# A decoder layer with 32 experts: two spare places for expert weights, emptied by GpSimd's copies

## The reference, cut to what matters

```python
SEQ, D_MODEL, N_EXPERTS, TOP_K = 256, 1024, 32, 4

def reference(x, c, positions, ...):
    mod = silu(c) @ ada_w + ada_b                  # six rows: shift, scale, gate, twice
    h = rms_norm(x) * (1 + scale1) + shift1
    x = x + gate1 * rms_norm(hybrid_mixer(h, ...))
    h = rms_norm(x) * (1 + scale2) + shift2
    x = x + gate2 * rms_norm(moe_ffn(h, ...))
    return x

def moe_ffn(h, ...):
    top_val, top_idx = top_k(h @ w_router + b_router, 4)
    weight = softmax(top_val)
    # for each expert e and its tokens:
    #   hu = h[tokens] @ w_up[e] + b_up[e]         # 1024 x 2048, 8 MB
    #   a  = clamped_swiglu(hu)
    #   out[tokens] += weight * (a @ w_down[e] + b_down[e])   # 1024 x 1024, 4 MB
```

## Time and profile before

| | us |
|---|---|
| median of 3 runs | 1294.62 (1293.81 to 1295.19) |
| the profiled execution | 1292.38 |
| its span, first to last instruction | 1290.2 |
| TensorE busy in the span | 1123.2 |
| SyncE's queue: 460.98 MB | 85.4% of the 16 DMA engines |
| VectorE, ScalarE, GpSimd busy | 316.0, 314.2, 0.2 |

### The profile page before, as it was taken

How to read it: one execution, slowest core, us unless ns; L and a number is a source line. 1 busy time by engine, 2 the same in 40 slices (tenths; PEclk the granted TensorE clock), 3 DMA queues, 4 the chain that set the end, 5 groups by cost and what they waited for, 6 DMA issues and landing times.

```text
span 1290.2 us, 20882 instructions
## 1 busy us (share of the span) xinstructions
PE 1123.2 (87%) x7942; PEld 569.1 (44%) x7943; DVE 316.0 (24%) x802; ACT 314.2 (24%) x589; POOL 0.2 (0%) x4
## 2 busy tenths in 40 slices
PE   6999999998998669988988989979978688687785
PEld 4745788753444233443343443433433334233332
DVE  3045463462221110312121211212111112111112
ACT  2145422032222221112122221222222122222213
POOL 0000000000000000000000000000000000000000
PEclk9999999998999889989999999999999899899898
DMA  9932664553899999469999999999999999999995
GB/s 381 428 130 98 275 279 186 216 217 151 315 419 428 428 428 370 177 240 429 426 429 428 429 428 428 429 428 430 427 430 429 429 427 428 430 427 429 429 429 249
DMA packets 33740, 464.89 MB, mean 360 GB/s; under 512 B 4002, under 2 KB 4130, under 8 KB 5540
## 3 DMA queue, kind: packets, MB, share of 16 engines
q1 hardware_dynamic: 32688, 460.98, 85.4%
q10 hardware_dynamic: 1012, 3.34, 0.7%
HBM read 463.25 MB, written 1.05 MB: 360 GB/s over the span
## 4 chain that ended last, share of the span: by engine, by line
PE 58%; DMA 37%; DVE 3%; issue 1%; SPq 0%; ACT 0%; DVEq 0%; ACTq 0%
DMA ring<-in_w_up 33%; PE psum L972 20%; PE psum L595 17%; PE psum L1049 8%; DMA ring<-in_w_down 3%; PE psum L900 3%; PE psum L964 2%; PE psum L1067 2%; DMA ring<-in_ada_quarters 1%; PE psum L661 1%; DVE area L1754 1%; PE psum L601 1%; PE psum L947 1%; DVE area L1725 0%; PE psum L891 0%
## 5 line engine op out<-in xcount | busy, mean ns | idle before, releaser
L972 PE MATMUL psum<-ring,area 128*32 128x512 f32 (+2 forms) x2432 | 391.3, 632 | 77.9 <-DMA ring<-in_w_up 77.9
L972 PEld LDWEIGHTS psum<-ring,area 128*32 128x32 f32 (+2 forms) x2432 | 107.3, 122 | 352.0 <-issue 228.7
L1049 PE MATMUL psum<-ring,area 128*32 128x256 f32 (+2 forms) x2080 | 191.3, 419 | 23.6 <-DVE area L1739 14.8
L900 PEld LDWEIGHTS psum<-area,x_res 128*128 128x128 f32 x1056 | 124.5, 196 | 33.8 <-issue 33.8
L900 PE MATMUL psum<-area,x_res 128*128 128x128 f32 x1056 | 131.2, 283 | 1.7 <-DVE area L1634 1.7
L1049 PEld LDWEIGHTS psum<-ring,area 128*32 128x32 f32 (+2 forms) x2080 | 75.9, 115 | 128.4 <-issue 66.3
L1260 ACT ACTIVATE area<-area 128x256 f32<-128x256 f32 x51 | 21.3, 417 | 420.5 <-DVE area L1714 420.5
L1714 DVE TENSOR_SCALAR area<-psum 128x256 f32<-128x256 f32 x51 | 21.7, 425 | 405.6 <-PE psum L972 405.6
L1219 ACT ACTIVATE area<-psum,mod,small 128x128 f32<-128x128 f32 (+1 forms) x272 | 101.7, 455 | 58.2 <-PE psum L900 55.1
L1248 ACT ACT_TABLE_LOAD x32 | 41.1, 1283 | 281.9 <-PE psum L947 281.9
L595 PE MATMUL psum<-ring,hT 128*128 128x512 f32 (+1 forms) x192 | 77.5, 559 | 0.0
(11 more groups left out here) (201 smaller groups left out, 632.9 us busy)
## 6 DMA issues: line engine op xcount, KB each, us to landing
ring<-in_w_up SPq DMA_DIRECT2D x128, 2048.0 KB, 22.2
ring<-in_w_down SPq DMA_DIRECT2D x64, 2048.0 KB, 22.5
ring<-in_w_in SPq DMA_DIRECT2D x10, 2048.0 KB, 16.0
ring<-in_ada_w SPq DMA_DIRECT2D x8, 2048.0 KB, 13.1
ring<-in_ada_quarters SPq DMA_DIRECT2D x4, 2048.0 KB, 18.0
ring<-in_w_out SPq DMA_DIRECT2D x2, 2048.0 KB, 10.0
ring<-in_w_in SPq DMA_DIRECT2D x4, 512.0 KB, 18.7
ring<-in_w_branch_b SPq DMA_DIRECT2D x1, 2048.0 KB, 9.3
```

Source lines behind the costliest of these rows:

```text
L900: ins = pe.matmul(ps[banks[i]][:, kk % 4 * P:(kk % 4 + 1) * P], x3[:, tt, kk * P:(kk + 1) * P], S[:, tt, 0:P], start=(tt == 0 and kk % 4 = ...
L972: ins = pe.matmul(ps[b][g * P // G:(g + 1) * P // G, 0:w], XT[:, kk, t0:t0 + P // G], wt[:, c0:c0 + w], start=False, stop=kk == KT - 1, sk ...
L1049: ins = pe.matmul(ps[b][g * M:(g + 1) * M, 0:w], hidT[:, p, q * P + of * M:q * P + (of + 1) * M], down_weights(kk)[:, g * W + d * CW:g * W ...
```

## The change

Two places of 2 MB are added, `extra[0]` and `extra[1]`. The first lies over `hT` and the start of `arena`, the second over another part of `arena` with `ybT` and `silu_rep`, which are not used in the expert loop; the tiles that the loop does use are moved behind (`S`, `Sg`, `GT`, `xw` and the router's), and `area` grows.

For places 1, 2, 7 and 8 the first two pairs of `w_up` are loaded into the spare places, and for places 1 and 7 both halves of `w_down` after them. GpSimd copies each into its slot of the ring once that is free, in eight copies of 128x512, and raises the semaphore that TensorE waits for anyway. Pairs 2 and 3 go to the ring directly as before, and so do all loads of the other places. `UP_BY_WAY` and `DOWN_BY_WAY` hold, for each such place, how many times the spare place was emptied before.

```diff
+UP_BY_WAY = {1: 0, 2: 2, 7: 3, 8: 5}
+DOWN_BY_WAY = {1: 1, 7: 4}
...
-        area = sb("area", TT * D + 14848)
+        area = sb("area", TT * D + KT * T + 14848 + 2048)
...
+        extra = [area[:, TT * D:TT * D + KT * CW], arena[:, 8192:8192 + KT * CW]]
...
+            un.wait_full(sp, "logit1")
+
+            def up_by_way(number, e):
                 for j in range(2):
+                    if UP_BY_WAY[e]:
+                        sp.wait_ge(extra_read[j], UP_BY_WAY[e])
+                    sp.dma_start(extra[j], a["w_up"][ds(number, 1), j, :, :].rearrange("e p n -> p (e n)")
+                                 ).then_inc(extra_full[j], 16)
+
+            def up_rest(number, e):
+                sp.wait_ge(up_used, (KT - 2) * e)
+                up_load(number, 2)
+                sp.wait_ge(up_full, MAX_U * e)
+                up_load(number, 3)
+
+            def down_by_way(number, e):
+                for j in range(2):
+                    sp.wait_ge(extra_read[j], DOWN_BY_WAY[e])
+                    sp.dma_start(extra[j], a["w_down"][ds(number, 1), j, :, :].rearrange("e p n -> p (e n)")
+                                 ).then_inc(extra_full[j], 16)
...
+            two_by_way(1)
+            direct(3, 7)
+            two_by_way(7)
+            direct(9, E)
...
+        @block.gpsimd
+        def _(gp):
+            def moved(j, to, landed):
+
+                for c in range(KT):
+                    ins = gp.tensor_copy(to[:, c * CW:(c + 1) * CW], extra[j][:, c * CW:(c + 1) * CW])
+                ins.then_inc(landed, 16)
+
+            for e in sorted(UP_BY_WAY):
+                for j in range(2):
+                    gp.wait_ge(extra_full[j], 16 * (UP_BY_WAY[e] + 1))
+                    gp.wait_ge(up_used, (KT - 2) * (e - 1) + 2 * j + 2)
+                    moved(j, slot(NF + j), up_pair[j])
+                    gp.wait_ge(up_pair[j], 16 * e + 16)
+                    gp.sem_inc(extra_read[j], 1)
+                if e not in DOWN_BY_WAY:
+                    continue
+                for j in range(2):
...
```

More of the change, by code:

```diff
@@ L207, in layer_kernel @@
         x_res = sb("x_res", TT * D)
-        hT = sb("hT", KT * T)
-        area = sb("area", TT * D + 14848)
+        area = sb("area", TT * D + KT * T + 14848 + 2048)
         yaT = sb("yaT", 2 * T)
-        ybT = sb("ybT", 4 * T)
         grow = sb("grow", D)
         late = sb("late", LATE_W)
-        silu_rep = sb("silu_rep", KT * 32)
         mod = sb("mod", 48)
@@ L222, in layer_kernel @@
         xn = area[:, 0:TT * D]
-        arena = area[:, TT * D:]
+        hT = area[:, TT * D:TT * D + KT * T]
+        arena = area[:, TT * D + KT * T:]
+        ybT, silu_rep = arena[:, 10752:10752 + 4 * T], arena[:, 11776:11776 + KT * 32]
+        extra = [area[:, TT * D:TT * D + KT * CW], arena[:, 8192:8192 + KT * CW]]
         cols = cst[:, C_COLS:C_COLS + R_N]
@@ L259, in layer_kernel @@
         sbT = region(8704, (8, T))
-        gates = region(10752, (16, T))
-        sbw = region(10752, (10, TRI))
+        gates = region(12288, (16, T))
+        sbw = region(12288, (10, TRI))
         prob = xn[:, 0:NG * P + NG * T]
@@ L289, in layer_kernel @@
         Y = hid
[L290 to L293, removed]
+        S = region(16384, (TT, T))
+        Sg = region(12288, (2, TT * P))
+        GT = region(12800, (2, T))
+        xw = region(13312, (8, T))
         pick = yaT[:, :].rearrange("p (c m) -> p c m", c=4)
[L295 to L303, removed]
+        lg = region(15360, (8, TT * E))
+        posm = region(15872, (TT, E + 1))
+        gate = region(15872 + 2 * (E + 1), (TT, E + 1))
+        top = region(15872 + 4 * (E + 1), (TT, 8))
+        posm2 = region(15872 + 4 * (E + 1) + 16, (TT, E + 1))
+        posm64 = rope[:, 0:TT * (E + 1)].rearrange("p (x y) -> p x y", x=TT)
+        gT = region(16128, (T,))
+        gate4 = region(13312, (TT, P))
         ada_sums = [grow[:, 0:CW], grow[:, CW:D]] + [region(i * CW, (CW,)) for i in (0, 1, 2, 3, 8, 9)]
@@ L350, in layer_kernel @@
         up_used, dn_used = sem("up_used"), sem("dn_used")
+        extra_full, extra_read = ([sem(f"{n}{j}") for j in range(2)] for n in ("extra_full", "extra_read"))
         xe_full, xe_read = sem("xe_full"), sem("xe_read")
@@ L563, in _ @@
             sp.wait_ge(order_ready, 1)
[L564 to L571, removed]
-                for j in range(2):
[L573 to L577, removed]
+            un.wait_full(sp, "logit1")
@@ new lines, in down_by_way, with down_direct @@
+            def down_by_way(number, e):
[3 more added lines that the diff above has]
+                                 ).then_inc(extra_full[j], 16)
+            def down_direct(number, e):
+                sp.wait_ge(dn_used, (FT // 2 - 1) * e - (FT // 2 - 1) + 2)
+                down_load(number, 0)
+                sp.wait_ge(dn_full, MAX_D * e)
+                down_load(number, 1)
@@ new lines, in direct, with two_by_way @@
+            def direct(first, last):
+                with sp.Fori(first, last) as e:
+                    number = expert_at(sp, e)
+                    for j in range(KT // 2):
+                        if j < KT // 2 - 1:
+                            sp.wait_ge(up_used, (KT - 2) * e - (KT - 2) + 2 * j + 2)
+                        else:
+                            sp.wait_ge(up_full, MAX_U * e)
+                        up_load(number, j)
+                    down_direct(number, e)
+            def two_by_way(first):
+                with sp.Fori(first, first + 1) as e:
+                    number = expert_at(sp, e)
+                    up_by_way(number, first)
+                    up_rest(number, first)
+                    down_by_way(number, first)
+                with sp.Fori(first + 1, first + 2) as e:
+                    number = expert_at(sp, e)
+                    up_by_way(number, first + 1)
+                    up_rest(number, first + 1)
+                    down_direct(number, first + 1)
@@ L581, in _ @@
             sp.wait_ge(stored, 16 * TT)
+        @block.gpsimd
[14 more added lines that the diff above has]
+                for j in range(2):
+                    gp.wait_ge(extra_full[j], 16 * (DOWN_BY_WAY[e] + 1))
+                    if j == 0:
+                        gp.wait_ge(dn_used, (FT // 2 - 1) * (e - 1) + 2)
+                    else:
+                        gp.wait_ge(dn_full, MAX_D * e)
+                    moved(j, slot(NF + 4 + j), dn_half[j])
+                    gp.wait_ge(dn_half[j], 16 * e + 16)
+                    gp.sem_inc(extra_read[j], 1)
         @block.tensor
@@ L1545, in _ @@
             logit_scale()
-            link(v.memset(arena[:, 14336:14336 + 4 * (E + 1)], 0.0))
+            link(v.memset(arena[:, 15872:15872 + 4 * (E + 1)], 0.0))
             link(v.memset(posm2, 0.0))
```

## The result

| | before | after |
|---|---|---|
| median of the runs compared, us | 1294.21 (1292.98 to 1295.19, 4 runs) | 1281.20 (1279.43 to 1282.46, 4 runs) |
| ratio, 95% interval | | 0.9899 (0.9882 to 0.9916) |
| profiled execution and its span, us | 1292.38, 1290.2 | 1281.97, 1279.8 |
| TensorE busy, us | 1123.2 | 1130.9 |

What follows compares the result with a forecast made beforehand. The prediction took the queue of 2 MB weight loads, full from 567.6 on, to set the end, so only earlier DMA idle time counts. 3.5 + 4.9 = 8.4 us, 1294.62 - 8.4 = 1286.2 us; range 1283.0 to 1292.5.

Steps and rivals of the forecast that it cites:

- C = 5.2 us: GpSimd's time to copy one 2 MB place: eight copies at 0.63 us, with 0.2 us to start.
- ScalarE's row: ScalarE's SBUF-to-SBUF pass of 128x512, 630 ns, chosen as the price of one GpSimd copy.
- C = 6.2: Copy time of a place by the skill's best case of 769 ns; gain 6.4 us instead of 8.4, time 1288.2.
- Places 1 and 2, 3.5 us: Front part: loads before place 3 through at 379.5 instead of 383.0, so the queue is 3.5 us ahead.
- Rivals 1 and 2: Copies in places 1, 2: 1.5 us each, place 2 waits, 1305, chance 0.08; 0.8 to 1.1 us, 1289 to 1294, 0.20.
- Places 7 and 8, 4.9 us: Loads fill the idle DMA stretch around place 6; the lead left at place 11's first load is 4.9 us.
- the queue is ahead by 6.3 us: Place 8's loads are through at 590.7 where before it was 597.0.
- The narrow point: Place 11's first load: its issue at 650.5 leaves the DMA 1.4 us idle, shrinking the lead to 4.9 us.
- the forecast's case with C = 3.4: Fast end of the forecast's case (C 3.4 to 6.5, chance 0.60): gain 10.4 us, 1284.2.
- rival 3: GpSimd's copies hold up VectorE's activations; places 1, 7 and 8 lose about 1 us each, 1288 to 1289; chance 0.07.
- the 1.7 us of cover: In place 7, the last activation ends at 574.15 and TensorE needs it at 575.88; two hold-ups would take 1.3 us.
- rival 4: SP stands at an earlier wait, or TensorE sets the pace after place 9: no change, 1294; chance 0.05.

Runs made afterwards that it cites:

- the group alone: Changed kernel with the spare places used only for places 1 and 2, loads from place 3 on as before: 1290.29 us, ratio 0.9970.
- The two kernels with one load moved: One load held until later: second half of w_down of place 7 in the kernel before, 1289.86 us; up pair 0 of place 8 in the changed kernel, 1284.54.
- w_down of place 7 direct: Changed kernel, but w_down of place 7 goes straight into the ring and up pairs 0 and 1 of place 8 to spare places ahead of it: 1284.72 us, 0.9931.
- slow copies: Changed kernel with each 2 MB place copied in 64 pieces of 128x64 instead of eight of 128x512: 1307.27 us, ratio 1.0105.

## Why the prediction failed, step by step

- **The copy, C = 5.2 us: right.** Eight copies take 4.5 to 4.9 us and the hand-over 0.2 to 0.4:

```profile
347.58 4.51 POOL L635 COPY ring<-area 128x512 f32<-128x512 f32 x8 [19.88 <-DMA area<-in_w_down]
352.47 4.68 POOL L635 COPY ring<-area 128x512 f32<-128x512 f32 x8 [0.38 <-DMA area<-in_w_down]
361.04 4.89 POOL L635 COPY ring<-area 128x512 f32<-128x512 f32 x8 [3.88 <-DMA area<-in_w_up]
366.56 4.51 POOL L635 COPY ring<-area 128x512 f32<-128x512 f32 x8 [0.63 <-DMA area<-in_w_up]
```

  These are both halves of w_down of place 1 and pairs 0 and 1 of place 2, the tight place. ScalarE's row was the right neighbour. The figure of the Trainium skill ("GPSIMD Engine Reference", elementwise cycle accounting) that gave C = 6.2 did not hold for this copy: 769 ns against 555 from start to start. The prediction took the less fitting figure of that section of the Trainium skill: 769 ns is for an unrolled loop, and for its shortest loop bodies (k up to 2) the section gives 1.03 cycles an element. By its 1.2 GHz that is an estimate of 0.86 ns; the copies here show 0.84. (With the 0.2 us to start, which the prediction left out there, its C would have been 6.4.)
- **Places 1 and 2, 3.5 us: right.** Up pair 0 of place 2 is issued at 352.34, 2.8 us later than the forecast's 349.5, in an execution whose place 1 starts 3.7 us later. The section is 3.7 us shorter, the group alone 4.0 us faster. TensorE never waits for GpSimd. Rivals 1 and 2 fell.
- **Places 7 and 8, 4.9 us: the failed step.** The prediction stood "in the times of before" and moved only loads. It had "pair 2 starts when its slot is free, at 571.1", taken from SyncE's timeline of before, and so "the queue is ahead by 6.3 us". It removed the w_down load from 552.45 and asked what the queue gained, not what else stood behind that load. TensorE's start of place 7 was a held-fixed number that depended on it: 2.5 us of wait and 2.7 us of slower matmuls. With both, the prediction's own reckoning closes. Pair 2 is on the DMA at 565.7, 5.4 us earlier than forecast (issued at 565.41), so the four loads are through at 565.7 + 4 x 4.89 = 585.3 where before it was 597.0: 11.7 us ahead. At place 11 the queue could start at 585.3 + 12 x 4.89 = 644.0, the issue comes at 644.81, some 1 us idle: 10.6 us ahead, and place 12 is 10.5 earlier. The narrow point was there as forecast, with about the forecast's loss (1.1 for 1.4).
- **The sum.** 3.5 + 4.9 + 2.5 + 2.7 = 13.6 for the 13.0 measured. The last two terms are read from one pair of profiles. The two kernels with one load moved put them together at 4.5 (from before) and 3.3 us (from after), by the ratios 3.5 and 3.4, a little under the 5.2; with pair 0 of place 8 held, place 7 is 2.0 us longer and not 2.7.
- **The range.** Its fast end was the forecast's case with C = 3.4. (1284.2 less 1 is 1283.2, not 1283.0; 1281.20 lies outside either.) It allowed for the unknown price of what the change adds, not for a second effect of what it takes away. The row that would have told it, 3.59 us of "issue" at the start of place 7, was in the trace of before, four rows ahead of the 575.88 of the earlier trace rows.
- **VectorE held up (rival 3): seen, and covered.** In place 7 the last steps of the activation run beside the copies of up pair 1 of place 8:

```profile
568.72 0.71 DVE L1799 SCALAR_TENSOR_TENSOR area<-area 128x256 f32<-128x256 f32 x1
...
570.53 0.38 PE L1083 MATMUL psum<-cst,area 128*128 128x128 f32 x2
```

  The step of 0.43 us takes 0.71, and 1.1 us of the 1.7 us of cover are left. TensorE goes on without a wait. The Trainium skill ("SBUF — State Buffer", who interferes with whom) states that such an instruction contends with a GpSimd copy; the trace agrees in kind. The hold-up is 0.28 us for this step, less than a whole copy, and GpSimd's slowest copy of the 96 is 0.81 us against a median of 0.61.
- **The loads don't come forward (rival 4): fell**, by the filled stretch at 533.8.

## What to carry to other kernels

Moving a transfer has two effects: the transfer is elsewhere, and what stood behind it on the DMA, here the fetch of an engine's code, is no longer held up. Before pricing such a move, look at every idle stretch marked "issue" on the engine that sets the pace, above all where it leaves one long code path for another, and ask which load was in flight there. Here a load that nobody needed soon was better issued clear of such a change, even though that meant later.

## What the runs showed of the hardware

- **Code behind weights.** With a 2 MB load issued 5.1 us before TensorE leaves place 6, TensorE waits 3.6 to 3.8 us (four programs, one of them twice); without it 0.95 to 1.5 us (six programs, two of them twice). With slow copies, one of the six, a load is issued 2.9 us before the leaving, some 0.2 us before the code packet, and the wait is 0.95 us. So what counts is a load already under way when the code is fetched. That is shown by taking a load away and putting one back; the order of the two inside the DMA engines, and how the wait goes with the size of either, was not tried.
- **The wait costs once more after it.** In the kernel before the granted clock falls at about 560.2, in the wait, and is 0.50 until 567.0. In 556 to 566 the granted clock is 0.71 in the kernel before and 1.00 in the changed one:

```profile
556.00:566.00 10.00, 6.41 (x30) 2.32 (x32) 1.25 (x4) 2.95 (x3) 0.00 (x0) 0.71 0.33 134
```

```profile
556.00:566.00 10.00, 8.94 (x78) 3.46 (x80) 1.25 (x4) 2.95 (x3) 5.15 (x10) 1.00 0.58 213
```

  It was 0.77 with places 1 and 2 alone, 0.83 with pair 0 of place 8 held and 0.70 with w_down of place 7 direct, three more with the long wait, and 1.00 in the kernel before with its load held. With the long wait part of that stretch is run at the lower of the two levels, 1.2 for 2.4 GHz, and place 7 takes 20.7 to 21.5 us in the five profiles. With the short wait it takes 18.6 to 18.7 in six and 19.5 and 19.6 in two, those last at a clock of 1.00 too, which stays unexplained.
- **A clock that differs from execution to execution in the front.** After 32 matmuls of one column the same code in 222 to 236 ran at a mean granted clock of 1.00, 0.88 or 0.76, the kernel before at 1.00 in one profile and 0.76 in another. The first row is the kernel before, the second the changed one:

```profile
222.00:236.00 14.00, 14.00 (x77) 12.01 (x78) 4.06 (x11) 5.53 (x6) 0.00 (x0) 1.00 0.86 354
```

```profile
222.00:236.00 14.00, 14.00 (x62) 11.66 (x62) 2.12 (x6) 5.56 (x6) 0.00 (x0) 0.76 0.87 355
```

  In the 13 profiles place 1 begins at 350.0 to 350.8 where this clock is 1.00 (five), at 352.1 to 352.7 where it is 0.88 (five) and at 353.6 to 354.2 where it is 0.76 (three), whatever the kernel. The kernel before has both ends, 349.98 and 353.65. That is why single profiles are compared by sections. What decides it was not tried.
- **GpSimd's copy, float32, from SBUF to SBUF.** 128x512 takes 0.555 us from start to start; 128x64 0.178 us (11.37 / 64, in the fastest groups). The line through both, an estimate, is 0.12 us an instruction and 0.84 ns an element of a partition.
